# Adding the gated expert outputs to x on GpSimd, and ScalarE's order of work, in one stage of a two-layer hybrid backbone

## What is computed

```python
# end of layer 0 (f: weighted sum of each token's two expert outputs)
x_ctx = x_ctx + mod_c[5] * f[bsz * n_lat:].reshape(bsz, n_ctx, d)
x_lat = x_lat + mod_l[:, 5] * f_lat.reshape(bsz, n_lat, d)
...
# start of layer 1
def rmsnorm(x, g):
    xf = x.astype(F32)
    y = xf * lax.rsqrt(jnp.mean(xf * xf, axis=-1, keepdims=True) + EPS)
    return (y * g.astype(F32)).astype(x.dtype)

def modulate(x, g, shift, scale):
    return rmsnorm(x, g) * (1.0 + scale) + shift
```

## Time and profile before

| | |
|---|---|
| median of 3 runs | 1602.69 us (1601.48 to 1606.28) |
| profiled execution, its own time | 1608.24 us |
| its span | 1606.3 us |
| PE busy | 1276.9 us, 79% |
| DVE busy | 602.9 us, 38% |
| ACT busy | 386.3 us, 24% |
| POOL busy | 35.3 us, 2% |
| bytes moved | 507.68 MB, 316 GB/s mean |
| the changed stage | 874.56 to 909.44 us of the span |

### The profile page before, as it was taken

The page is one execution under the profiler, slowest core; times in us unless marked ns, Lnnn a source line. Parts: engine busy times, 40 slices in busy tenths (PEclk is TensorE's granted clock), DMA queues, the critical chain, the costliest instruction groups (busy, mean ns, idle before and its releaser), DMA issues. The chain is left out here.

```text
span 1606.3 us, 36190 instructions
## 1 busy us (share of the span) xinstructions
PE 1276.9 (79%) x14878; PEld 733.0 (46%) x14879; DVE 602.9 (38%) x1630; ACT 386.3 (24%) x812; POOL 35.3 (2%) x79
## 2 busy tenths in 40 slices
PE   4898887987699997867764599879799886666766
PEld 3355654544465554434432446645355543333333
DVE  1528565435422221211210547665634333122212
ACT  1244233213122222221210422543211111101101
POOL 0200101000000000000001000000000000000000
PEclk8899898998799998998987699979899999888888
DMA  8620996536899999999997620053879999999997
GB/s 318 218 81 12 335 384 238 220 158 249 338 429 416 428 428 429 429 429 430 428 429 286 222 105 0 1 224 160 347 317 427 427 428 428 429 428 428 429 429 300
DMA packets 81810, 507.68 MB, mean 316 GB/s; under 512 B 13293, under 2 KB 17746, under 8 KB 56394
## 3 DMA queue, kind: packets, MB, share of 16 engines
q1 hardware_dynamic: 74712, 489.21, 74.2%
q10 hardware_dynamic: 3906, 8.83, 1.4%
q0 software_dynamic: 3120, 8.63, 1.4%
HBM read 494.61 MB, written 12.03 MB: 315 GB/s over the span
## 5 line engine op out<-in xcount | busy, mean ns | idle before, releaser
L1621 PE MATMUL bank<-sb_ring,sb_scratch 128*32 128x256 f32 x2240 | 143.5, 414 | 53.8 <-DMA sb_ring<-in_moe_w_up 44.9
L1803 PE MATMUL bank<-sb_ring,sb_scratch 128*32 128x256 f32 x1664 | 119.8, 451 | 70.6 <-DMA sb_ring<-in_moe_w_up 66.7
L1702 DVE TENSOR_TENSOR sb_scratch<-sb_scratch,bank 128x128 f32<-128x128 f32 x50 | 14.4, 288 | 321.4 <-ACT sb_scratch L1655 321.4
L1621 PEld LDWEIGHTS bank<-sb_ring,sb_scratch 128*32 128x32 f32 x2240 | 77.0, 119 | 118.4 <-issue 79.8
L1803 PEld LDWEIGHTS bank<-sb_ring,sb_scratch 128*32 128x32 f32 x1664 | 64.3, 129 | 125.1 <-issue 105.3
L1659 ACT ACTIVATE sb_scratch<-bank 32x256 f32<-32x256 f32 x200 | 75.0, 375 | 162.1 <-PE bank L1631 160.4
L1883 DVE TENSOR_TENSOR sb_scratch<-sb_scratch,bank 128x128 f32<-128x128 f32 x38 | 10.9, 288 | 249.9 <-ACT sb_scratch L1839 249.9
L1601 PE MATMUL bank<-sb_h,sb_scratch 128*32 128x256 f32 x1632 | 99.2, 384 | 3.3 <-DVE sb_scratch L1689 3.3
L1839 ACT ACTIVATE sb_scratch<-bank 128x128 f32<-128x128 f32 x38 | 10.5, 278 | 373.6 <-PE bank L1803 373.6
L1803 PE MATMUL bank<-sb_scratch 128*32 128x256 f32 x768 | 56.7, 461 | 29.0 <-DMA sb_scratch<-in_moe_w_up 27.3
L1621 PE MATMUL bank<-sb_scratch 128*32 128x256 f32 x960 | 60.2, 407 | 22.9 <-DMA sb_scratch<-in_moe_w_up 20.2
(11 more groups left out here) (400 smaller groups left out, 1903.5 us busy)
## 6 DMA issues: line engine op xcount, KB each, us to landing
sb_ring<-in_moe_w_gate SPq DMA_DIRECT2D x44, 2048.0 KB, 27.4
sb_ring<-in_moe_w_up SPq DMA_DIRECT2D x44, 2048.0 KB, 31.9
sb_ring<-in_moe_w_down SPq DMA_DIRECT2D x41, 2048.0 KB, 34.4
sb_ring<-in_ada_w SPq DMA_DIRECT2D x21, 2048.0 KB, 16.6
sb_scratch<-in_moe_w_gate SPq DMA_DIRECT2D x20, 2048.0 KB, 28.6
sb_scratch<-in_moe_w_up SPq DMA_DIRECT2D x20, 2048.0 KB, 32.3
sb_scratch<-in_moe_w_down SPq DMA_DIRECT2D x20, 2048.0 KB, 34.1
sb_ring<-in_cd_w_in SPq DMA_DIRECT2D x4, 2048.0 KB, 9.2
```

What stands on the lines that cost most here:

```text
L1621: last = nc.tensor.matmul(c.bank(1, 2, FQ)[MB * q:MB * q + MB, :, :], m.xt[:, k, :], m.gu[j][:, :, k, q * FQ:(q + 1) * FQ], start=k == 0, ...
L1702: v.tensor_tensor(m.hm, m.sg, c.ps[1][:, FQ:2 * FQ], ALU.mult).then_inc(hm_ready, 1)
L1803: last = nc.tensor.matmul(c.bank(1, 2, FQ)[MB * q:MB * q + MB, :, :], m.xt[:, k, :], m.gu[j][:, :, k, q * FQ:(q + 1) * FQ], start=k == 0, ...
```

## The change

In `combine_norm_stage` the third operation of `add` (x plus the gated y0) moves from DVE to POOL, behind POOL's eight gathers, with a new semaphore from DVE to POOL. ACT's list becomes weigh 0, 1, square 0, weigh 2, square 1, root 0, weigh 3, square 2, eviction of stream 0's bank 0, square 3, root 1, then the other evictions. ACT takes one root of `eps` into an unused column at the start. DVE does add 3 before scale 0.

```diff
--- before.py
+++ after.py
@@ -1905,7 +1905,8 @@
     W = LT * P
     ss, eps = c.stat[:, 0:NT], c.stat[:, NT:NT + 1]
     modcol = cut(c.scr, 2 * D, 2, 2, KC)
-    gate_in, gathered, weighed, added = S("moe_gate_in"), [S(f"rows_gathered{t}") for t in tiles], S("first_rows_weighed"), S("rows_added")
+    gate_in, gathered, weighed, gated, added = (
+        S("moe_gate_in"), [S(f"rows_gathered{t}") for t in tiles], S("first_rows_weighed"), S("rows_gated"), S("rows_added"))
     cols_in, eps_set, means, roots, scaled, turned, act_evicted, dve_evicted = (
         S(x) for x in ("mod_columns_in", "eps_set", "square_means", "roots_ready", "rows_scaled", "x_turned", "ht_even", "ht_odd"))
     with nc.Block() as block:
@@ -1927,6 +1928,9 @@
                     pool.indirect_dma_start(m.pair[:, t, k, :], None, c.sorted_out,
                                             bass.IndirectOffsetOnAxis(ap=c.slot[:, k * NT + t:k * NT + t + 1], axis=0)
                                             ).then_inc(gathered[t], 16)
+            for t in tiles:
+                pool.wait_ge(gated, t + 1)
+                nc.gpsimd.tensor_tensor(c.x[:, t, :], c.x[:, t, :], m.pair[:, t, 0, :], ALU.add).then_inc(added, 1)
 
         @block.scalar
         def _(act):
@@ -1939,33 +1943,34 @@
                 nc.scalar.activation(c.h[:, t, :], c.x[:, t, :], ACT.Square, scale=D ** -0.5, accum_out=ss[:, t:t + 1]).then_inc(means, 1)
 
             def root(s):
-                if s == 0:
-                    act.wait_ge(eps_set, 1)
                 act.wait_ge(means, (s + 1) * LT)
                 of_stream = ss[:, s * LT:(s + 1) * LT]
                 nc.scalar.activation(of_stream, of_stream, ACT.Sqrt, bias=eps).then_inc(roots, 1)
 
-            def evict(s):
-                for b in (0, 2):
-                    act.wait_ge(turned, 4 * s + b + 1)
-                    for k in (2 * b, 2 * b + 1):
-                        last = nc.scalar.activation(c.ht[:, k, s * W:(s + 1) * W], c.bank(4 + b, 2, W)[:, k % 2, :], ACT.Identity,
-                                                    bias=modcol[:, s, 0, k:k + 1], scale=modcol[:, s, 1, k:k + 1])
-                    last.then_inc(act_evicted, 1)
-
+            def evict(s, b):
+                act.wait_ge(turned, 4 * s + b + 1)
+                for k in (2 * b, 2 * b + 1):
+                    last = nc.scalar.activation(c.ht[:, k, s * W:(s + 1) * W], c.bank(4 + b, 2, W)[:, k % 2, :], ACT.Identity,
+                                                bias=modcol[:, s, 0, k:k + 1], scale=modcol[:, s, 1, k:k + 1])
+                last.then_inc(act_evicted, 1)
+
+            act.wait_ge(eps_set, 1)
+            nc.scalar.activation(c.stat[:, NT + 1:NT + 2], eps, ACT.Sqrt)
             weigh(0)
             weigh(1)
+            square(0)
             weigh(2)
-            square(0)
             square(1)
             root(0)
             weigh(3)
+            square(2)
             act.wait_ge(cols_in, 16 * len(streams))
-            square(2)
-            evict(0)
+            evict(0, 0)
             square(3)
             root(1)
-            evict(1)
+            evict(0, 2)
+            evict(1, 0)
+            evict(1, 2)
 
         @block.vector
         def _(dve):
@@ -1975,8 +1980,7 @@
                 dve.wait_ge(weighed, t + 1)
                 y0, y1 = m.pair[:, t, 0, :], m.pair[:, t, 1, :]
                 step(v.scalar_tensor_tensor(y0, y1, c.wsel[:, NT + t:NT + t + 1], y0, ALU.mult, ALU.add))
-                step(v.tensor_tensor(y0, y0, m.gate[:, t // LT, :], ALU.mult))
-                v.tensor_tensor(c.x[:, t, :], c.x[:, t, :], y0, ALU.add).then_inc(added, 1)
+                v.tensor_tensor(y0, y0, m.gate[:, t // LT, :], ALU.mult).then_inc(gated, 1)
 
             def scale(s):
                 of_stream = ss[:, s * LT:(s + 1) * LT]
@@ -1998,8 +2002,8 @@
             add(0)
             add(1)
             add(2)
+            add(3)
             scale(0)
-            add(3)
             dve.wait_ge(cols_in, 16 * len(streams))
             evict(0)
             scale(1)
```

## The result

The changed kernel takes 1614.01 us (median of 8 runs, 1608.69 to 1616.15), the kernel before 1603.13 us (median of 8, 1601.48 to 1608.06). The ratio of the runs side by side is 1.0046, 95% interval 1.0033 to 1.006, which is 7.4 us of 1603 (5.3 to 9.6). The prediction was 1609.3 us, or +6.6, in a range of 1602.0 to 1612.0. The median of the changed kernel's runs lies 2 us above the range's upper end, but it is 10.9 us over the median of before, more than the paired ratio gives. The ratio, times the median of 1602.69 us that the prediction started from, is 1610.1.

A forecast was written before the change was run, and what follows sets the result against it. VectorE was taken as the stage's critical engine. Without overlap, its 10.3 us plus 8.8 us of GpSimd additions put scale 0 at 904.1; the 11.93 us tail made +6.6 us, from 1602.69 to 1609.3 us, range 1602.0 to 1612.0.

The forecast's parts named there:

- The stage sets what the whole loses: At the join to the next stage: whatever the stage gains or loses is passed on whole to all that follows.
- The table load is hidden: ScalarE, ahead of root 0: the 1.28 us load ran while VectorE was adding, so moving it earlier gains nothing.
- The fixed tail of 11.93 us: From scale 0's start to the next stage's first product: 11.93 us, against 13.12 before.
- The addition takes 2.2 us: GpSimd's addition of x per tile: taken as 2.2 us, between bounds of 1.81 and 2.67.
- No overlap: VectorE's operations beside GpSimd's additions: they run as one engine, 10.3 plus 8.8 us from 885.02; chance 0.66.
- Addition 3 gets in ahead of scale 0: Last GpSimd addition lands before VectorE's scale 0 and holds it; if scale 0 went first, the loss would be +4.4 us.
- The sum: Scale 0 at 904.1 plus the tail of 11.93: stage ends at 916.1 instead of 909.5, 6.6 us longer.
- case "slower": Whole kernel measurably slower, by more than about 0.3%, 4.8 us; chance 0.53.
- two rivals with partial or no exclusion: On VectorE: only scale held up, +2.4 us, chance 0.14; nothing held up, +0.3 us, chance 0.16.
- ScalarE's order: ScalarE's new order of weighs and squares, feeding VectorE's tiles 2 and 3: adds no wait.

The follow-up runs named there:

- root_first: Kernel before with only the extra root at the start; work part (VectorE's first weighted sum to the next stage's first product) 24.46 us, as before.
- dve_add: Changed kernel with x's addition put back on VectorE; stage 37.47 us, work part 27.00 us, ratio to the kernel before 1.0017.
- pairs: Kernel before plus a stage where GpSimd runs one operation beside twelve short VectorE ones, in several operand forms; GpSimd's addition took 2.34 us in company and alone.
- psum_operands: Changed kernel with weighed and gate rows in PSUM, so VectorE's sums and gatings have one SBUF and one PSUM input; stage 38.33 us, ratio to before 1.0018.
- apart: psum_operands with weigh 2, 3, square 3 and root 1 earlier, root in PSUM, stream 0 scaled by ScalarE, a later VectorE eviction; ratio to before 0.9972.
- pairs 3 and 6: In the added stage of pairs, GpSimd's addition (3) or VectorE's two SBUF inputs beside zeroing's rival form, one SBUF input (6); longest VectorE operation 2.48 and 1.92 us.
- weigh_ahead: Changed kernel, but ScalarE weighs tile 2 before square 0 and tile 3 before square 1; stage 40.17 us, work part 29.95 us, ratio to before 1.0041.
- pool_only: Kernel before with only x's addition moved to GpSimd, old orders kept; stage 38.77 us, work part 27.87 us, ratio to before 1.0019.

## Why the prediction was right, and where its size came from

- **The stage sets what the whole loses.** Right. The stage was 5.72 us longer, and the time behind it changed by 0.79.
- **The table load is hidden.** Right: root_first has the stage of before to 0.01 us. After shows it at 876.07, 9.45 us before the first weighing, and none ahead of root 0.
- **The fixed tail of 11.93 us.** Right in its mechanism; too long by 0.80. In dve_add scale 1 comes 5.87 us after scale 0 (taken: 5.86), and the next stage 6.08 us after scale 1 (taken: 6.07). In the changed kernel scale 0 ran unheld from 903.46 + 3.52 - 1.42 = 905.56, and the next stage began 11.13 us later. What the term didn't have is the clock, which rose behind the transposes of stream 0 and made those of stream 1 0.81 us shorter.
- **The addition takes 2.2 us.** It took 2.34, between the bounds of 1.81 and 2.67. (The Trainium skill, GPSIMD Engine Reference, section Performance versus the Vector engine: 4497 ns for 2048 values, an estimate of 2.25 for half of them; the measured value is 0.09 above.)
- **No overlap.** Right, shown by the holds in the timeline, by pairs, and by psum_operands, where the holds vanish with the operands. From the first sum to the unheld start of scale 0 I had 19.12 us (10.32 + 8.8); it was 18.78. VectorE's own part was 9.9 instead of 10.3, since the step from a gating to the next tile's sum takes 1.16 us and not 1.25 (889.26 - 888.10). Four additions of 2.34 are 0.56 us more than forecast. That this didn't show is because the held operation's own work begins 0.14 to 0.21 us before the record of the addition ends.
- **Addition 3 gets in ahead of scale 0.** Right: it started at 903.43, scale 0 at 903.46.
- **The sum.** +6.6 us forecast, +5.45 in the work part, +7.4 (5.3 to 9.6) in the paired runs. Against the work part the forecast is 1.1 us too large: 0.80 is the clock, 0.34 the 19.12 against 18.78. That it lies so near to the paired +7.4 is in part luck. The profile has only 5.45 us in the work part, 0.27 in the gathers and 0.79 behind the stage, one execution doesn't show whether the clock rose in the others, and the rest isn't located; the interval's lower end, 5.3, would leave nothing to locate. That end also lies over the 4.8 us that the prediction took as the least it could tell from no change, so its case "slower" (0.53) came true.

What the prediction didn't tell apart is how the loss is made up. It named exclusion as the cause and put the order of add 3 and scale 0 into the tail as if it gained 1.2 us there. By its own numbers, four tiles of 3.78 us and a tail of 11.93 give 27.05 us without GpSimd, 2.6 more than before: the order alone loses, and dve_add measured 2.54. GpSimd brought the other 2.91 us. The two rivals with partial or no exclusion had the same tail in them; they came out at +2.4 and +0.3 because a free GpSimd would have taken 4.9 us of additions away from VectorE. Both are refuted by the same rows.

ScalarE's order, which the prediction said adds no wait, did add 1.18 and 0.23 us of idle time on VectorE. These lay beside additions 1 and 2, and were covered: taking them away changed the work part by 0.04 us, or by 0.57 up to scale 0.

## What to carry to other kernels

Before moving work from VectorE to GpSimd, list the operands of everything that runs beside it: a GpSimd operation that reads SBUF and a VectorE operation with two inputs in SBUF (or one, in the form of pairs 3 and 6, which takes 0.29 us from SBUF and 0.42 from PSUM) run one after the other, so the move adds the slower engine's time instead of taking the faster one's away. If VectorE's other operand comes from PSUM, nothing is held and the move can win: apart did, though psum_operands, which kept the orders and scale 0 as they were, still lost 3.27 us. And look for waiting inside records as well as between them, by comparing the duration of one form with its usual one; and ask of every reordering what had filled the wait that it empties.

## What the runs showed of the hardware that was not expected

- A held operation has its waiting in its own record (a 0.43 us operation at 2.62). No view of waits shows it.
- Two configuration instructions of GpSimd that the kernel doesn't write stand ahead of its first addition. They cost nothing: in pairs they took 0.01 us each at 873.8, and the first addition began at 873.91 with VectorE's first operation and took 2.34 us like the others.
- GpSimd copies 1024 float32 values per partition in 1.03 us, close to its zeroing (0.95) and less than half its addition (2.34). VectorE needs 1.22 us for a like addition.
- ScalarE's table load took 1.28 us, and the root behind it began at once (893.81, 895.10); no other cost of the switch was seen.
- TensorE's clock rose in the changed stage behind the transposes of stream 0 (0.94 while TensorE paused, 910.28 to 912.32), and in weigh_ahead only during those of stream 1 (0.50 until 908.90, 1.00 from 910.70; transposes at 3.62 us). In dve_add and pool_only it stayed at 0.50, with transposes at 3.82. The work of TensorE was the same in all; what makes the clock rise there wasn't tried.
